# Two-layer block on one Trainium2 core: what is worked out beside the second expert call stays in SBUF, on half of that call's ring

## The reference, cut to what matters

```python
p = xn @ wl                       # q, k, v, pool, conv input, b, c, gates
q = apply_rope(qk_heads(p[..., Q_OFF:K_OFF], q_norm_g[l]), cos, sin)
k = apply_rope(qk_heads(p[..., K_OFF:V_OFF], k_norm_g[l]), cos, sin)
o = blocked_diff_attn(q, concat([k, kc]), concat([v, vc]), lam)
pool = pool_branch(p[..., POOL_OFF:CIN_OFF], pool_w[l], pool_scale[l])
conv = conv_branch(h_part, b_gate, c_gate, conv_w[l], conv_out_w[l])
merged = g[:, :, 0] * attn + g[:, :, 1] * pool + g[:, :, 2] * conv
...
u = u_emb[eidx]                   # 128 experts a token, 1024 wide
hid = gelu(einsum('td,thkd->thk', xc, u))
out = einsum('thk,thkd->td', gate * hid, v_emb[eidx])
```

## Time and profile before

| what | us |
|---|---|
| three runs: median (least to most) | 3555.59 (3553.64 to 3556.43) |
| the profiled execution, its own time | 3549.04 |
| its span, first to last instruction | 3547.7 |
| mean granted clock of PE | 0.877 of full speed |

### The profile page before, as it was taken

The page is one execution under the profiler, slowest core; times in us unless marked ns, Lnnn a source line. Parts: engine busy times, 40 slices in busy tenths (PEclk is TensorE's granted clock), DMA queues, the critical chain, the costliest instruction groups (busy, mean ns, idle before and its releaser), DMA issues.

```text
span 3547.7 us, 31233 instructions
## 1 busy us (share of the span) xinstructions
PE 2832.3 (80%) x11602; PEld 1273.5 (36%) x11602; DVE 1984.5 (56%) x4447; ACT 371.7 (10%) x940; POOL 1546.7 (44%) x1587
## 2 busy tenths in 40 slices
PE   7999888778888868677777778978655655789998
PEld 4485446233543324332323222545300001125454
DVE  0051258788766645966666641666877776423233
ACT  1000231021000000100000001141000000002112
POOL 0010003666555566566666663102677777630000
PEclk9999999877999988888978888999777556999999
DMA  7275327999999999999999998726999999972332
GB/s 288 90 281 194 121 83 292 373 385 383 412 412 408 393 399 411 357 413 412 413 412 413 412 414 354 281 97 253 403 409 409 409 409 410 408 284 95 134 140 83
DMA packets 261713, 1130.77 MB, mean 319 GB/s; under 512 B 29749, under 2 KB 37141, under 8 KB 242489
## 3 DMA queue, kind: packets, MB, share of 16 engines
q0 software_dynamic: 221184, 805.40, 57.5%
q1 hardware_dynamic: 36312, 315.97, 22.7%
q10 hardware_dynamic: 4064, 7.41, 0.5%
HBM read 1120.20 MB, written 8.46 MB: 318 GB/s over the span
## 4 chain that ended last, share of the span: by engine, by line
DMA 35%; PE 33%; DVE 19%; POOL 7%; issue 4%; ACT 1%; SPq 0%; DVEq 0%; ACTq 0%
DMA big<-in_u,xT 20%; DMA big<-in_v,xT 12%; DVE big L2681 7%; POOL big L2753 6%; PE ps L2866 5%; PE ps L250 5%; PE ps L2450 4%; PE ps L1075 3%; PE ps L2348 2%; PE ps L732 2%; PE ps L1194 1%; PE ps L1183 1%; DMA bc<-in_w_mod 1%; DVE small L986 1%; PE ps L1769 1%
## 5 line engine op out<-in xcount | busy, mean ns | idle before, releaser
L2681 DVE CUSTOM_DVE_ANT_0 big<-big,ps 128x1024 f32<-128x1024 f32 x768 | 929.4, 1216 | 558.2 <-DMA big<-in_u,xT 550.0
L2450 PE MATMUL ps<-big,bc 128*32 128x512 f32 x3072 | 783.8, 770 | 449.0 <-DMA big<-in_v,xT 432.1
L2753 POOL DMA_INDIRECT big<-in_u,xT x768 | 736.7, 959 | 429.1 <-issue 147.8
L2753 POOL DMA_INDIRECT big<-in_v,xT x768 | 735.0, 957 | 428.8 <-PE ps L2450 170.2
L2450 PEld LDWEIGHTS ps<-big,bc 128*32 128x32 f32 x3072 | 103.2, 120 | 969.3 <-DMA big<-in_v,xT 818.9
L250 PE MATMUL ps<-w,xT 128*128 128x512 f32 x512 | 226.0, 602 | 2.8 <-ACT xT L529 1.2
L2866 PE MATMUL ps<-w,xT 128*128 128x512 f32 x416 | 184.3, 601 | 3.0 <-DMA w<-in_w_in 2.2
L2348 PE MATMUL ps<-tmp,w 128*128 128x256 f32 (+1 forms) x832 | 170.5, 365 | 10.2 <-DMA w<-in_peer_wq 5.2
L600 POOL TENSOR_TENSOR small<-small 128x32 f32<-128x32 f32 (+1 forms) x8 | 33.2, 4156 | 299.1 <-DVE small L571 238.8
L2348 PEld LDWEIGHTS ps<-tmp,w 128*128 128x128 f32 x832 | 146.4, 196 | 35.4 <-DMA w<-in_peer_wq 6.0
L250 PEld LDWEIGHTS ps<-w,xT 128*128 128x128 f32 x512 | 97.8, 193 | 125.3 <-issue 120.5
(11 more groups left out here) (388 smaller groups left out, 3277.6 us busy)
## 6 DMA issues: line engine op xcount, KB each, us to landing
w<-in_w_in SPq DMA_DIRECT2D x56, 2048.0 KB, 10.4
bc<-in_w_mod SPq DMA_DIRECT2D x19, 2048.0 KB, 10.1
w<-in_w_conv SPq DMA_DIRECT2D x24, 1536.0 KB, 9.2
w<-in_peer_wq SPq DMA_DIRECT2D x12, 2048.0 KB, 10.3
w<-in_w_out SPq DMA_DIRECT2D x10, 2048.0 KB, 7.8
w<-in_conv_out_w SPq DMA_DIRECT2D x6, 2048.0 KB, 10.2
big<-in_u,xT POOLq DMA_INDIRECT x768, 14.0
big<-in_v,xT POOLq DMA_INDIRECT x768, 17.9
```

The costliest lines, as they stand in the source:

```text
L2450: ins = pe.e.matmul(self.ps[to:to + 32, 2 + half, :], p["diag"][part % 2][:, 256 * g + 32 * m:256 * g + 32 * m + 32], self.ring_row(slots[ ...
L2681: dve.inc(dve.e.tensor_tensor_reduce(out=row, in0=row, in1=p["xc"], scale=1.0, scalar=0.0, op0=ALU.mult, op1=ALU.add, accum_out=p["hid"][t ...
L2753: ins = pool.e.indirect_dma_start(self.ring_row(slot), None, table, bass.IndirectOffsetOnAxis(index, 0))
```

## The change

`big` tiles 0 and 1 (slots 0 to 7) become the place where the second layer's q, k, v and pool columns are kept. At positions 44, 118, 192 and 268 of peer01 the plan takes two slots from the ring (j and 4 + j for j = 0 to 3), so that it has 14, 12, 10 and then 8. ACT copies each turn's projections straight there; before turns 0, 2, 4 and 6 it waits for the last consumers of the two slots (`kept_emptied`). The stores and the reading back of `ahead` and `ahead_gate` are gone; gates stay in `tmp` and `tmp2`, and the convolution's product goes to `bb`.

In turns 4 to 7 DVE normalizes and rotates q and k of one tile each, and POOL computes one power for it, all beside the call. After the six blocks, which come in another order, PE makes the banded and the pool products, still beside the call; their weights (1 MB each) are loaded there too. The side program's total grows from 276 to 294 units, of which a turn keeps 24. In `layer1` remain the context's k and v, their norm, the applying of the gates and the modulation columns. DVE's last sum of peer01 also waits for PE's last pool product, because the pool weights lie in the buffer that it writes.

```diff
-AHEAD_TURN, AHEAD_GATE = 24, 14
+AHEAD_TURN = 24
+AHEAD_WORK = (("gate", 2), ("gate", 3), ("out", 0), ("out", 1), ("gate", 0), ("gate", 1), ("band", 0), ("pool", 0))
+AHEAD_SHARE = {"gate": 14, "out": 14, "band": 9, "pool": 9}
+KEPT_FROM = (44, 118, 192, 268)
+ROPE_TURN = 4
...
-        self.norm_rope_sp(sp, 1)
-        sp.wait_ge(self.proj_out, "ahead proj", 7)
-        self.ahead_in.inc(sp.e.dma_start(self.big[:, 0:2, :], self.d["ahead"].rearrange("t p n -> p t n")), "ahead in")
+        self.load_row(sp, 3, self.d["pool_scale"][1:2, :], "pool scale", 1, dst=self.pool_scale1())
         kv(2)
         self.mod_load(sp, 17, 2)
         kv(3)
-        self.mod_load(sp, 18, 2)
-        sp.wait_ge(self.proj_out, "ahead gate", 4)
-        sp.wait_ge(self.conv_out_sem, "ahead gate", 5)
...
-        self.ahead_gate_sp(sp, 0)
-        sp.wait_ge(self.act, "norm11", "squares")
-        self.ahead_gate_sp(sp, 1)
-        self.band_sp(sp, 1)
-        self.mod_load(sp, 19, 2)
-        self.mod_load(sp, 20, 0)
-        self.mod_load(sp, 21, 2)
...
-        self.load_row(sp, 3, self.d["pool_scale"][1:2, :], "pool scale", 1, dst=self.pool_scale1())
-        for c in range(2):
-            sp.wait_ge(self.dve, self.gated1(2), "merge", c, 1)
-            self.ahead_gate_sp(sp, 2 + c)
-            self.mod_load(sp, 22 + c, 2 - c)
+        for n, slot in ((18, 2), (19, 2), (20, 0), (21, 2), (22, 1), (23, 0)):
+            self.mod_load(sp, n, slot)
...
-        self.mod_pe(pe, 20)
-        self.band1_pe(pe)
-        pe.wait_ge(self.w_in[0], "w", self.gated1(1), "product", 0)
-        pe.wait_ge(self.act, "band", 1, "out", 1)
-        self.mod_pe(pe, 21)
-        self.pool1_product_pe(pe, 0)
-        self.mod_pe(pe, 22)
-        self.pool1_product_pe(pe, 1)
-        self.mod_pe(pe, 23)
+        for n in range(20, 24):
+            self.mod_pe(pe, n)
...
-        self.norm_act(act, "norm11", [2, 3])
-        act.inc(act.e.copy(self.xT[:, :, 0:SEQ], self.aheadT()))
+        for i in range(2):
+            act.inc(act.x.activation(self.merged[:, 3, :], self.h[:, 2 + i, :], ACT.Square, accum_out=self.small[:, 8 + i:9 + i]))
+        act.mark("norm11", "squares")
+        act.inc(act.e.copy(self.xT[:, :, 0:SEQ], self.aheadT()), "ahead xT")
...
+        dve.wait_ge(self.act, "ahead xT")
+        halves = lambda a: a.rearrange("p (j n) -> p j n", j=2)
+        for c in range(2):
+            self.gate1_dve(dve, c)
+            for i in range(2):
+                dve.inc(dve.x.tensor_tensor(halves(self.merged[:, i, c * BANK:(c + 1) * BANK]), self.conv_product(c, i),
+                                            halves(self.ahead_rows(c)[:, i, :]), ALU.mult))
         for tile in range(2):
             dve.wait_ge(self.act, "kv1", "out", 1, tile)
-            self.heads_norm_dve(dve, 1, 2 + tile, self.tmp2)
-        for c in range(2):
-            self.gate1_dve(dve, c)
+            self.heads_norm_dve(dve, 1, 2 + tile, self.big[:, 2, 0:D].rearrange("p (a n) -> p a n", a=2))
+        dve.wait_ge(self.row_in[3], "row", "pool scale", 1)
         for c in range(2):
             cols = slice(c * BANK, (c + 1) * BANK)
+            self.gate1_dve(dve, 2 + c)
+            sg = self.ahead_rows(2 + c)
+            dve.inc(dve.x.tensor_tensor(sg, sg, self.pool_scale1()[:, cols].unsqueeze(1).broadcast_to((P, 2, BANK)), ALU.mult))
             for i in range(2):
...
+                g, m = sg[:, i, :], self.merged[:, i, cols]
+                dve.inc(dve.x.tensor_tensor(g, self.ba(i)[:, cols], g, ALU.mult))
+                dve.inc(dve.x.tensor_tensor(m, m, g, ALU.add))
...
+        for w, (kind, g) in enumerate(AHEAD_WORK[:6]):
+            yield self.ahead_work_at(w, 0)
+            src = self.w_cols(1, GATE_OFF + (2 - g // 2) * D + g % 2 * BANK) if kind == "gate" else self.columns("conv_out_w", 1, g)
+            self.load_w(sp, w % 2, [(self.wk(w % 2), src)], ("ahead", "work", 2 * w + 1), "ahead work", w)
+            if w == 3:
+                sp.wait_ge(self.pe, "peer01", "scores", STEPS - 1)
+                sp.wait_ge(self.dve, "ahead", "convolved", KC - 1)
+                self.band_sp(sp, 1)
+                sp.wait_ge(self.dve, "peer01", "summed h", 0)
+                self.ahead_in.inc(sp.e.dma_start(self.ahead_pool_w(), self.d["pool_w"][1].rearrange("p (g k n) -> p g k n", g=4, k=2)), "pool w")
...
+    def ahead_rows(self, g):
+        return (self.tmp2 if g >= 2 else self.tmp)[:, 2 * (g % 2):2 * (g % 2) + 2, :]
...
+        band = self.bc[:, 4:6, :].rearrange("p a (w t) -> p a w t", w=4)
+        pe.wait_ge(self.band_in, "band", 1)
+        pe.wait_ge(self.act, "ahead", "copied", KC - 1)
+        for n in range(4):
+            yield self.ahead_work_at(6, n / 4)
...
+            pe.inc(ins, "ahead", "work", 12 + n)
+        pooledT, pw = self.ahead_pooledT(), self.ahead_pool_w()
+        pe.wait_ge(self.ahead_in, "pool w")
+        for n in range(4):
+            c, i = n // 2, n % 2
+            yield self.ahead_work_at(7, n / 4)
+            pe.wait_ge(self.act, "ahead", "emptied", 12 + 2 * c + 1)
+            bank = self.ahead_take(pe, 16 + n)
...
+            pe.inc(ins, "ahead", "work", 16 + n)
...
+                if kind == "gate":
+                    act.inc(act.e.activation(self.ahead_rows(g)[:, i, :], src, ACT.Tanh, scale=0.5), "ahead", "emptied", use)
                 else:
...
+                    act.wait_ge(self.pe, "peer01", "scores", STEPS - 1)
+                    act.inc(act.e.copy(self.conv_product(g, i), src.rearrange("p (j n) -> p j n", j=2)), "ahead", "emptied", use)
+        for n in range(4):
+            yield self.ahead_work_at(6, (n + 1.2) / 4)
+            act.wait_ge(self.pe, "ahead", "work", 12 + n)
...
+        for n in range(4):
+            c, i = n // 2, n % 2
+            yield self.ahead_work_at(7, (n + 1.2) / 4)
+            act.wait_ge(self.pe, "ahead", "work", 16 + n)
+            act.inc(act.e.copy(self.ba(i)[:, c * BANK:(c + 1) * BANK], self.ps[:, 5 + (16 + n) % 3, :]), "ahead", "emptied", 16 + n)
...
-            if turn:
-                act.wait_ge(self.proj_out, "ahead proj", turn - 1)
+            if turn % 2 == 0:
+                self.kept_emptied(act, turn // 2)
             for i in range(2):
                 act.wait_ge(self.pe, "ahead", "proj", turn, i)
-                act.inc(act.e.copy(self.tmp2[:, i, :], self.ps[:, 6 + i, :]))
+                act.inc(act.e.copy(self.big[:, i, turn * BANK:(turn + 1) * BANK], self.ps[:, 6 + i, :]))
             act.mark("ahead", "copied", turn)
-            yield self.ahead_at(turn, 20 / 40)
-            act.wait_ge(act, "ahead", "copied", turn)
-            dst = self.d["ahead"].rearrange("t p n -> p t n")[:, :, turn * BANK:(turn + 1) * BANK]
-            self.proj_out.inc(act.e.dma_start(dst, self.tmp2[:, 0:2, :]), "ahead proj", turn)
...
+            if turn >= ROPE_TURN:
+                yield from self.ahead_rope_dve(dve, turn)
...
+        a, tile = divmod(turn - ROPE_TURN, 2)
+        ss = self.small[:, 256:272]
+        sq = self.tmp2[:, 0:2, :].rearrange("p a (s d) -> p (a s) d", d=64)
+        x = self.big[:, tile, a * D:(a + 1) * D].rearrange("p (s d) -> p s d", d=64)
...
+        yield self.ahead_at(turn, 1 / 40)
+        dve.wait_ge(self.act, "ahead", "copied", 2 * a + 1)
+        dve.inc(dve.x.tensor_tensor(sq, x, x, ALU.mult))
+        yield self.ahead_at(turn, 3 / 40)
+        dve.inc(dve.x.reduce_sum(ss, sq, AX_X))
+        dve.inc(dve.x.tensor_scalar(ss, ss, 1.0 / 64, EPS, ALU.mult, ALU.add), "ahead", "rope mean", turn)
+        yield self.ahead_at(turn, 14 / 40)
+        dve.wait_ge(self.pool, "ahead", "rope rstd", turn)
+        dve.inc(dve.x.tensor_tensor(x, x, ss.unsqueeze(2).broadcast_to((P, 16, 64)), ALU.mult))
...
+        dve.inc(dve.x.tensor_tensor(x2, x2, s2, ALU.add))
+    def ahead_rope_pool(self, pool):
+        ss = self.small[:, 256:272]
+        for turn in range(ROPE_TURN, KC):
+            yield self.ahead_at(turn, 8 / 40)
+            pool.wait_ge(self.dve, "ahead", "rope mean", turn)
+            pool.inc(pool.e.tensor_tensor(ss, ss, self.minus_half.broadcast_to((P, 16)), ALU.pow), "ahead", "rope rstd", turn)
...
+            if stream and at in KEPT_FROM:
+                free = [(slot, before) for slot, before in free if slot >= 8 or slot % 4 != KEPT_FROM.index(at)]
...
+    def kept_emptied(self, lane, j):
+        order, name = self.peer_order(), "peer01"
+        for kept in (j, 4 + j):
+            kind, e = order[max(at for at, (slot, _) in enumerate(self.plan_of[0, 1]) if slot == kept)]
+            if kind == "u":
+                lane.wait_ge(self.dve, name, "dot", e)
+            else:
+                lane.wait_ge(self.pe, name, "sum", e // 2)
...
+            dve.wait_ge(self.pe, "ahead", "work", 19)
...
+        together(self.peer_pool(pool, 0, 1), [(52, 512, self.ahead_rope_pool(pool.beside()))])
```

(5 more changed lines are left out.)

174 lines of the change are left out of this document (66 added, 108 removed).

## The result

| | before | after |
|---|---|---|
| median of 13 runs (lowest to highest), us | 3553.64 (3544.92 to 3566.39) | 3567.22 (3557.73 to 3571.18) |
| ratio of the two, 95% interval | | 1.0039 [1.0030, 1.0049] |
| profiled execution, its span, us | 3549.04, 3547.7 | 3567.27, 3565.5 |
| SP loads peer01's gate row (L226 `bc<-mods`), us | 1418.41 | 1427.34 |
| SP's first issue behind peer01 (L217 `bc<-in_w_mod`) | 2195.76 | 2228.15 |

The changed kernel is slower, by 13.6 us or 0.39%. The forecast was 3550 us, faster; the time lies inside its range and on the wrong side.

The account below looks back on a forecast made before the run. DMA bytes were taken to bound peer01, and a chain through DVE's norms `layer1`. -17.4 + 5.1 - 10 + 9 + 6 + 2 = -5.3 us from the profiled 3549.04 gave 3543.7, or 3550 for the median; range 3533 to 3580.

Parts of the forecast that it names:

- POOL's power and its wait: In four turns of peer01, POOL waits for DVE's mean, then computes a 2.9 us power: +2 us, 0 to 12.
- The ring: In peer01, eight slots cost 3.4% of the time gathers run alone, positions 268 to 511: +9 us, 0 to 21.
- The stores: In peer01, thirteen stores gone free 2.6% of 670 us of DMA time, the bound there: -17.4 us.
- DVE's rotation: In turns 4 to 7 of peer01, added operations take DVE to 81% and lower the DMA rate: +6 us, 0 to 13.
- PE in the call: In peer01, PE hides the added banded and pool products: 0, range 0 to 4 us.
- The stage: In `layer1`, the modulation weights' load ends the chain, no longer DVE's norms: -10 us, range -8 to -12.
- B: Rival: in peer01's stretches without weight loads, positions 268 to 511, the eight-slot ring starves; +14 us, 3570; chance 0.28.
- A: Rival: eight slots hold in peer01, all costs together below 8 us; -14 to -22, middle -18, 3538 us; chance 0.27.
- D: Rival: in peer01, DVE's rotation operations on two SBUF operands hold up POOL's gathers; 11 us, 3561 us; chance 0.03.
- loads: Band and pool weights, 1 MB each, are now loaded in peer01 at 412 GB/s: +5.1 us.

Follow-up runs that it names:

- E1: The changed kernel with POOL's power for the rotation moved from 8/40 to 18/40 of its turn and DVE's products squeezed in after it; 3548.33 us, 0.9989 of before.
- E2: The changed kernel with the norm and rotation of q and k taken back behind the call, into the stage; 3542.33 us, 0.9968 of before.
- E3: The kernel before with only peer01's ring cut to eight slots, two each at positions 44, 118, 192, 268; stores stay; 3560.17 us, 1.0019 of before.
- E6: The kernel before with each of the call's fourteen stores issued twice, 7.3 MB more on ACT's queue; 3564.45 us, 1.0039 of before.
- E12: The kernel before with its ring cut to eight slots and four unused 16-column powers on POOL, without added waits; 3570.30 us, 1.0059 of before.
- E4: The changed kernel without the rotation's eight products and sums per turn; square, sum, mean, POOL's wait and power stay; 3563.48 us, 1.0030 of before.
- E5: E2 with PE's banded and pool products and ACT's copies of them also moved behind the call, loads staying; 3541.29 us, 0.9977 of before.

## Why the prediction was wrong, and where it was right

**The step that failed is "POOL's power and its wait": +2 us, with bounds of 0 and 12.** Moving the power out of the wait's reach shortens the call by 15.3 us (after against E1). The call of after is 21.5 us longer than E2's, which has all of the change but the rotation; the forecast had 8 us for that, 2 here and 6 for DVE. The text had every piece: that POOL may run only 4.7 positions ahead there, and that all later gathers queue behind the wait. It then priced the power's own 2.9 us alone, four times, as the upper bound, and never the wait.

The wait has to be worked out in two sums; I do it here afterwards, and only from rows of before and the timeline above. The first is the hole in the issues. The row that the mean stands behind is asked for six gathers, some 8 us, before POOL stops. It lands after 12 us with ten slots and after about 7 with eight; behind it come two dots (4.0 us with what belongs to them in the timeline above), 2.6 us of square, sum and mean and 2.9 of power. That is 12 - 8 + 4.0 + 2.6 + 2.9 = 13.5 us in the first two turns and 8.5 in the other two, 44 in all; measured are 14.2, 10.4, 10.7 and 4.9, 40 in all, so the sum is right in total and off by up to 4 us in a turn. The second is what the rows on their way cover: landing over interval, 12 / 1.5 = 8 rows with ten slots and 7 / 1.5 = 4.7 with eight, at 1.27 us each 10.2 and 5.9 us. So 3.3 and 2.6 us are left per turn, 12 us in all instead of 2, and the sum would have come out some 4 us slower instead of 5 faster: the sign turns, but barely. What the rows of before didn't show is the start of the engines after each pause, 1.6 to 2.2 us, 7 us in four turns. Together that is 19 us, and the engines were idle 19.0.

The reason that kept it at nothing, that weights of the convolution load at that place, is refuted by the first of the 10 us windows, 172 GB/s, and by SP's queue, which moved 0.02 MB in that hole. The prediction's own sign, a DMA share below 0.95 within 10 us after the power, is met in all four turns (0.51, 0.56, 0.46 and 0.81 in the 10 us windows).

**The ring, +9 us (0 to 21): right in size, wrong in place.** 7.2 in the call, 7.1 by the medians (E3). The forecast took 3.4% of the stretches in which gathers run alone. But after's four quarters from 2000 us on have 409 to 414 GB/s; the loss falls mostly between 1750 and 2000 us, where the side turns run and E3 has 398 GB/s. Why there and not later the runs don't say, and that the two sizes agree is in part luck. This stretch alone makes 9 us of lost DMA time (250 x (1 - 398/413)), more than the 7.2 us by which the call grows. That fits the end of the call, where before's engines have a share of 0.32 from 2180 to 2190 us while PE finishes; this was argued, not tested.

**The stores, -17.4 us: mechanism right, size a little high.** 14.5 us for 7.3 MB (E6), so about 13.5 for the 6.82 MB. The share of engines' time that the queue shows (2.6%) overstates it; bytes over rate gave 16.5.

**DVE's rotation, +6 us (0 to 13): not confirmed, though a number agrees.** E1 against E2, the rotation with its power but without the wait, is 6.0 us by the medians and 6.3 in the call. But the power is in it, and four powers without a wait cost 5.6 us or more by themselves (E12). By E4 the products have little part in it, at most 4 us by the medians and nothing in the call; DVE reached 71% in after and 74% in E1, not 81. As far as these runs tell, most of the 6 us is the power's, and DVE's operations cost little.

**PE in the call, 0: right** (E5: 2.0 us in the call, too little to tell from nothing).

**The stage, -10 us (-8 to -12): right in kind, -13.3 measured, just outside its bounds.** The chain ends with the modulation weight, as said. E2 shows that most of it doesn't come from the rotation's place: with the norms behind the call the stage is still 97.3 us.

**The rivals.** B's sign came true by another mechanism: the ring didn't starve between weight loads, it was emptied four times by one instruction. A was nearer on the ring than on the whole. D is refuted as a large effect by E4, and a gather's issue between 1700 and 1930 us takes 0.944 us at the median in after against 0.941 in before. The Trainium skill's rule of "DMA: Bandwidth & Descriptors", section "Anatomy of one DMA — SWDGE (gpsimd) path", which I had worked out as an estimate of 3.2 us for a gather, doesn't fit the landings here: 7.2 us with eight slots, and 6.1 to 6.4 with six, though the engines were no longer full there (366 GB/s). Even the gathers that after issues into idle engines, at 1733.63 and 1863.51 us, land in 4.4 and 4.3 us, the first in the DMA view from 1733.6 to 1734.5 us:

```profile
big<-in_u,xT POOLq DMA_INDIRECT x1, 4.4
```

The measurement decides.

**The sum again, with measured terms:** stores -13.5, loads +5.1, ring +7.2, rotation with wait and power +21.5, stage -13.3: +7 us. The call and the stage of the two executions give +10.2, the medians +13.6. E2's call is 1.9 us over before's, where the terms without the rotation give -1.2: 3 us of that difference stay open. Of the 21.5 the wait is 15.3 by E1, and 6.3 are the power and DVE's operations; how these two share it, and why the engines' 19.0 us of pauses are fewer than 21.5, stays open too.

**What stays.** The change without the rotation in the call (E2) is 0.32% faster than before (0.9958 to 0.9978): keeping the products in SBUF was worth its ring.

## What to carry to other kernels

An instruction put on the queue that issues the gathers is priced by the hole it leaves in the issues: from the last gather ahead of it, over the landing of the rows that its operand's engine must first consume, to its own end; the rows then on their way (landing over interval) are taken off, the start of the engines after a pause (1.6 us here) is added, and the rest is paid each time. Place such a wait at least a whole ring behind the instruction that it waits for (here, with ten and eight slots, the wait was gone at 14 positions, and 7.5 and 4.7 cost 7 and 15 us of the call), or leave the work where no gathers queue behind it; the instruction's own time isn't free even without a wait (E12). For a shorter ring, work out slots x interval - landing - (issue and hold): it told that eight slots nearly hold and six don't. The size of the loss it gave only with a rate read from other rows, 9 us for 7 at eight slots and 58 for 52 to 59 at six.

## What the runs showed of the hardware that I had not expected

Landing time follows the rows on their way, not the transfer: 20.6 us with sixteen slots, 12 with ten, 7.2 with eight, all at 409 to 414 GB/s, 6.1 to 6.4 with six at 366 GB/s, and 4.3 to 4.4 into idle engines. In these runs a long landing is a queue that is full, and no cost. After a pause the first bytes flow 1.6 us after the gather's issue begins. And executions of the same code differ by up to 12 us before they reach the changed part (1418.4 to 1430.3 us at the same instruction), which is nearly as much as the whole effect of 13.6: pieces have to be compared from a mark inside the execution.
